# Hybrid decoder layer: where the transposes stand around the two output products of a token tile

## What is computed

```python
mix = merge_groups(h, om, att, g_m, g_a, w_out)      # rms_norm of both groups, then y @ w_out (1024 x 1024)
xp = layer_norm(DN_ALPHA * xp + mix, ln1_g, ln1_b)
...
logits = (xf @ w_router + b_router).astype(F32)      # 1024 x 32
top_v, top_i = lax.top_k(logits, TOP_K)
gates = jax.nn.softmax(top_v, axis=-1)
```

## Time and profile before

| | |
|---|---|
| time before, median of 3 runs | 1549.62 us (1548.44 to 1549.96) |
| the profiled execution, device time | 1550.05 us |
| its span, on which the trace's times stand | 1547.9 us |
| PE busy | 1383.3 us, 89% |
| DVE busy | 437.3 us, 28% |
| the loop over tiles 1 to 4 | 355.2 us to 434.9 us of the span |

### The profile page before, as it was taken

The page is one execution under the profiler, slowest core; times in us unless marked ns, Lnnn a source line. Parts: engine busy times, 40 slices in busy tenths (PEclk is TensorE's granted clock), DMA queues, the critical chain, the costliest instruction groups (busy, mean ns, idle before and its releaser), DMA issues.

```text
span 1547.9 us, 32726 instructions
## 1 busy us (share of the span) xinstructions
PE 1383.3 (89%) x12980; PEld 683.3 (44%) x12980; DVE 437.3 (28%) x1014; ACT 326.9 (21%) x758; POOL 311.8 (20%) x328
## 2 busy tenths in 40 slices
PE   7999899789879999988899999899998988999980
PEld 5778676574542433333334343233442333343330
DVE  2311534545564221221212212111321112211125
ACT  1102001361001322213222222221322212232120
POOL 5223200111231212111121112211112111122012
PEclk9999997669867999999999999999999999999996
DMA  9245000305046999999999999999999999999953
GB/s 303 61 89 122 21 35 23 97 25 211 28 151 237 398 409 402 410 413 410 411 402 405 412 409 410 404 408 408 402 412 405 409 408 405 405 401 408 417 205 115
DMA packets 100515, 460.85 MB, mean 298 GB/s; under 512 B 30482, under 2 KB 40862, under 8 KB 51200
## 3 DMA queue, kind: packets, MB, share of 16 engines
q1 hardware_dynamic: 81440, 426.48, 68.3%
q0 software_dynamic: 18336, 30.14, 7.8%
q10 hardware_dynamic: 592, 2.13, 0.4%
HBM read 442.21 MB, written 22.37 MB: 300 GB/s over the span
## 4 chain that ended last, share of the span: by engine, by line
PE 59%; DMA 20%; DVE 11%; SPq 5%; issue 3%; ACT 1%; POOL 0%; ACTq 0%; DVEq 0%; POOLq 0%
PE PS L1369 19%; DMA ring<-in_w_moe_dram 19%; PE PS L1391 14%; PE PS L1032 6%; PE PS L1044 6%; PE PS L1273 4%; SPq L489 3%; DVE mix L1927 2%; PE PS L1382 1%; PE PS L1351 1%; DVE qmT L1932 1%; DVE qmT L1934 1%; SPq L497 1%; PE PS L1361 1%; DVE qmT L1928 1%
## 5 line engine op out<-in xcount | busy, mean ns | idle before, releaser
L1369 PE MATMUL PS<-ring,mix 128*32 128x512 f32 x5376 | 605.1, 597 | 53.3 <-DMA ring<-in_w_moe_dram 42.4
L1369 PEld LDWEIGHTS PS<-ring,mix 128*32 128x32 f32 x5376 | 164.7, 110 | 453.3 <-issue 345.2
L769 POOL DMA_INDIRECT expert_rows<-mix,smalls x84 | 112.4, 1338 | 798.2 <-issue 511.4
L1927 DVE TENSOR_TENSOR mix<-PS,kn 128x512 f32<-128x512 f32 x84 | 58.1, 691 | 573.1 <-PE PS L1369 567.8
L960 ACT ACTIVATE mix<-PS,smalls 32x256 f32<-32x256 f32 x336 | 156.6, 466 | 179.5 <-PE PS L1391 176.4
L1391 PE MATMUL PS<-ring,mix 128*32 128x256 f32 x3328 | 187.0, 380 | 0.0
L1391 PEld LDWEIGHTS PS<-ring,mix 128*32 128x32 f32 x3328 | 104.7, 110 | 69.5 <-issue 0.5
L944 ACT COPY mix<-PS 128x512 f32<-128x512 f32 (+1 forms) x48 | 24.0, 535 | 466.0 <-PE PS L1361 466.0
L1032 PE MATMUL PS<-ring,xT 128*128 128x256 f32 (+1 forms) x400 | 97.7, 407 | 2.4 <-issue 2.2
L760 POOL DMA_INDIRECT mix<-x_rows,smalls x84 | 86.7, 1032 | 59.5 <-issue 52.9
L1044 PE MATMUL PS<-xT,ring 128*128 128x280 f32 x384 | 96.0, 413 | 0.0
(11 more groups left out here) (372 smaller groups left out, 1009.5 us busy)
## 6 DMA issues: line engine op xcount, KB each, us to landing
ring<-in_w_moe_dram SPq DMA_DIRECT2D x320, 1024.0 KB, 19.4
xT<-in_w_moe_dram SPq DMA_DIRECT2D x32, 1024.0 KB, 23.8
X<-in_w_moe_dram SPq DMA_DIRECT2D x32, 1024.0 KB, 27.2
ring<-in_w_in_dram SPq DMA_DIRECT2D x9, 1024.0 KB, 10.8
ring<-in_w_out_dram SPq DMA_DIRECT2D x4, 1024.0 KB, 4.8
X<-in_x_prompt_dram SPq DMA_DIRECT2D x4, 512.0 KB, 5.7
ring<-in_state_mlstm_C_dram POOLq DMA_DIRECT2D x1, 2048.0 KB, 16.3
ring<-in_w_in_dram SPq DMA_DIRECT2D x8, 256.0 KB
```

Of the source, the lines that this page charges most:

```text
L769: nc.gpsimd.indirect_dma_start(out=y_dram, out_offset=bass.IndirectOffsetOnAxis(ap=lists[a][0:32, g, 1:2].bitcast(U32), axis=0), in_=ysb[g ...
L1369: ins = mm(bank(BANK0[a] + g)[32 * t:32 * t + 32, :], xgT[XBUF[a][g]][:, P * (k % 2) + 32 * (k // 2):P * (k % 2) + 32 * (k // 2) + 32], sl ...
L1927: link(V.tensor_tensor(ht, bank(BANK0[a] + g), b1b, ALU.add))
```

## The change

Inside the loop, on PE, `turn_rows(i + 1)` moves from behind the second half product to between the two, and `turn_x1(i - 1)` moves from behind it to its middle, after four of its eight blocks. `logits(i - 1)` stays behind the second half. On DVE the two copies that answer to these, and with them `gates_by_expert`, are put in the same order: both copies stand ahead of the second half's residual. The two calls of `turned_x1` and `turn_x1` behind the loop stay. The count of instructions is the same; `project` takes the blocks to do as an argument and counts `op_mm` with the last of them.

```diff
-            def project(i, half):
+            def project(i, half, part=range(KT)):
...
                 else:
-                    for k in range(KT):
+                    for k in part:
                         ins = mm(bank(2 + 2 * (i % 2) + half), mixT[i % 2][:, k, :],
                                  rowpair((s0 + k // 2) % STREAM)[:, k % 2, 512 * half:512 * half + 512],
                                  start=(k == 0), stop=(k == KT - 1))
-                ins.then_inc(op_mm, 1)
+                if KT - 1 in part:
+                    ins.then_inc(op_mm, 1)
...
                 project(i, 0)
                 if i >= 2:
                     rank_tokens(i - 2)
-                project(i, 1)
                 if i < NT:
                     turn_rows(i + 1)
+                project(i, 1, range(KT // 2))
                 turn_x1(i - 1)
+                project(i, 1, range(KT // 2, KT))
                 logits(i - 1)
...
                 residual_half(i, 0)
                 if i >= 2:
                     give_places(i - 2)
+                if i < NT:
+                    turned_rows(i + 1)
+                turned_x1(i - 1)
+                if i >= 2:
                     gates_by_expert(i - 2)
                 residual_half(i, 1)
                 centre(i)
-                if i < NT:
-                    turned_rows(i + 1)
-                turned_x1(i - 1)
                 normalise(i)
                 choose(i - 1)
```

## The result

| | before | after |
|---|---|---|
| median | 1549.79 us (4 runs) | 1535.51 us (1533.29 to 1536.75, 4 runs) |
| ratio | | 0.9908, 95% interval 0.9891 to 0.9925 |
| profiled execution, device time | 1550.05 us | 1533.29 us |
| its span | 1547.9 us | 1531.1 us |

The gain of the medians is 14.3 us; 14.1 were forecast. One execution each of three kernels further down took far longer (2.1, 5.0 and 7.6 ms): the ratios leave it out, the medians printed there hold it and would be 0.3 to 1.4 us lower without it. The two profiled executions lie 16.8 us apart, so not all of their difference is the change. To see what is, I cut both traces at the same three events: the start of the first product of the loop, the end of the last one (read at the start of the next group on PE), and the start of the product with the second bias.

A forecast was written before the change was run, and what follows sets the result against it. The prediction took PE's 9.5 us of waits for DVE's copy of the turned X, and the clock lost with them, as the bound. Loop 13.17 - 0.30 breaks + 1.26 behind it = 14.1 us gained: median 1535.5, range 1533.3 to 1542.5.

The forecast's parts named there:

- The bound: PE before the logits: waits for DVE's copy of X; a full tile pays gap, half-clock logits and slow next product.
- Tile 1: First, small-logits turn of the loop on PE: loses only its gap, 1.89 us.
- Tile 2: Second turn of the loop on PE: 22.12 us becomes 17.51, 4.61 less.
- Tile 3: Third turn of the loop on PE: 23.60 us becomes 17.60, 6.00 less.
- Tile 4: Last turn of the loop on PE, to the end of its products: 15.80 us becomes 15.13, 0.67 less.
- Logits at full clock: A full tile's logits on PE without the gap: taken as 1.60 us, between bounds of 1.44 and 1.81.
- The allowance of 0.3 us for breaks: Four more breaks in the products on PE, each a fresh start of 0.05 to 0.1 us: 0.3 us lost.
- The waits in the middle: PE's transposes inside the second half product: wait 0 to 0.2 us in tile 4; rival of 1 us per tile, 1539.5, chance 0.05.
- Behind the last product: DVE's chain after the loop: copy of X leaves it, LayerNorm and router 1.26 us earlier, POOL's root stays hidden.
- The expert stage: After the router: everything later hangs on the last product and DVE's chain, so the shift counts in full.
- The fall of the clock: Rival on PE in tiles 2 and 3: broken-up products lose full clock, 6.9 us given back, 1542.4; chance 0.11, whole or part.
- The slower rival: PE stays at 0.50 through all products from the first break on: 45 us more, less the 14, 1580 us; chance 0.03.

## Why POOL's root took a microsecond longer

In before, and with only the rows moved, or only PE's order, a copy out of PSUM stood on DVE while POOL made the reciprocal root, and line 718 took 0.57 us in the full tiles. With only X moved it took 0.56, 0.56 and 0.57 us in the tiles whose copy of rows stands there, and 1.58 in the last, where there is none. In the change it is 1.56 to 1.58 in every full tile. The small tile, which never had a copy there, has 1.46 in both kernels. One more kernel keeps DVE still while POOL works.

```diff
                 link(V.tensor_scalar(nbias[0:r], bag[0:r, 0:1], -1.0, None, ALU.mult))
-                link(V.scalar_tensor_tensor(z, z, nbias[0:r], lng[0:r, :], ALU.add, ALU.mult))
                 dve.wait_ge(ln_pow, i + 1)
+                link(V.scalar_tensor_tensor(z, z, nbias[0:r], lng[0:r, :], ALU.add, ALU.mult))
```

> The change, but DVE waits for POOL's reciprocal root ahead of the first step of the LayerNorm instead of ahead of the second, so DVE touches no rows while POOL works. Theory (DVE's full-width step on SBUF slows POOL's line 718 from 0.57 us to 1.57, and so the copy from PSUM that used to stand there was a cover): line 718 takes 0.57 us in all four full tiles. DVE then waits about 0.9 us and does both steps of 1.28, 3.6 us from the statistics to x1_done where the change has 3.4, so the bias product starts 22.3 us after the last output product instead of 22.1. Rival (line 718 is slow for a reason of its own): 1.57 again, and 23.3 us.

Measured: 1533.62 us in one run. Line 718 takes 0.54 us for the small tile and 0.56 to 0.57 for the others, and the bias product starts 22.5 us after the last output product (417.69 to 440.17), where the change has 22.1. The rows of DVE in the last tile, then POOL's:

```profile
419.66 0.15 DVE L1770 TENSOR_SCALAR smalls<-smalls 128x1 f32<-128x1 f32 x1
420.67 1.33 DVE L1772 SCALAR_TENSOR_TENSOR X<-X,smalls,kmT 128x1024 f32<-128x1024 f32 x1 [0.86 <-POOL smalls L718]
```

```profile
419.99 0.57 POOL L718 TENSOR_TENSOR smalls<-smalls 128x1 f32<-128x1 f32 x1
```

The cause is shown: DVE's 1.28 us step that reads X and the LayerNorm's gain, both in SBUF, makes POOL's 0.57 us instruction wait one microsecond. The Trainium skill (SBUF — State Buffer, SBUF: two separate sides) says that a DVE instruction with two SBUF inputs and a GpSimd instruction that reads SBUF lock each other out for the length of the one that came first; the trace agrees: DVE's step starts first, at 419.50, POOL's at 419.64, and POOL's ends 0.43 us behind DVE's, after 1.57 us instead of 0.57. Waiting first avoids the lock but not the time: it costs 0.4 us more.

## Why the prediction was right, step by step

- **The bound.** The three prices of a full tile (gap, logits at half clock, slow start of the product) are all gone. Right, and shown by undoing the parts.
- **Tile 1.** 1.89 us forecast, 1.75 measured (17.91 before, 350.75 to 366.91 after).
- **Tile 2.** 17.51 us forecast, 17.60 measured (366.91 to 384.51).
- **Tile 3.** 17.60 forecast, 17.67 measured (384.51 to 402.18).
- **Tile 4.** 15.13 forecast, 15.17 measured (402.18 to 417.35).
- **Logits at full clock.** I took 1.60 from bounds of 1.44 and 1.81; they took 1.71 us. The upper bound halved the length of the row, 3.62; half of the time from its start to the next one's, 3.43 (391.83 to 395.26 in the earlier trace rows), is 1.71. The allowance of 0.3 us for breaks covered the difference: the loop came out at 66.60 where the forecast has 66.56. The single breaks were cheaper than the allowance: two half products and the transposes between them take 4.31 + 3.43 us (392.73 to 397.04 to 400.47), and 6.95 + 0.87 is 7.82, against 7.74 measured.
- **The waits in the middle.** The place that tile 4's transposes wait for was done at 412.86 and PE came to it at 413.01. The slack was 0.15 us, the forecast had a wait between 0 and 0.2. No wait shows in the trace. This is the step with the least room; in tiles 2 and 3 about 1.0 us is left. The copy of X was there 1.9 us before the logits (398.54 and 400.47 in tile 3) and not 1.2: it began 0.3 us into the last four blocks, not 0.9.
- **Behind the last product.** Here a step failed, though the forecast came out. The prediction read POOL's root as done 0.94 us behind the statistics "so it stays hidden". But 0.57 us was its time beside a copy out of PSUM, and the change takes just that copy away. The row of the small tile in the earlier trace rows already held the answer: there line 1771 waits 0.52 us for line 718, with no copy ahead. Mis-sized by 0.54 us: 0.73 gained instead of 1.26.
- **The expert stage.** Counted as shifting in full; it does, apart from the 1.2 us that its length grew by.
- **The rivals.** The fall of the clock did not come. Its cause was not excluded by the rows I gave, though: the logits three times over show that a busy PE can lose it. Its price was a little high: in before, the logits and the products behind them take 6.4 us more than at full clock, where I had 6.9. The waits in the middle came within 0.15 us. The slower rival did not occur either, but its row, the bias product at half clock, turned out to be worth 7.1 us in its stage, of which 4.9 reach the next.

That the medians differ by 14.3 us and the forecast by 14.1 is luck in the last microseconds. By the stretches of the two traces the change brings 13.6 us up to the bias product, 12.8 and 0.7, and loses 1.2 behind it. The medians add to that what chance gives: the runs of the change alone lie 3.5 us apart.

## What to carry to other kernels

Where two engines work through lists in order and one waits for the other's copy, move the producer's transposes into the middle of a long product and the copy ahead of the next thing that waits for that product; do both, since the first alone made this kernel about 10 us slower. Before you move an instruction away, look at what ran on other engines beside it: it may have been the cover of one of them. When a stretch is busy and still at half clock, look at the shape of its products before you look for idle time.

## What the runs showed of the hardware that I had not expected

- The granted clock fell from 1.00 to 0.50 3.9 and 3.3 us into 6.7 and 7.3 us of gapless logits (128 rows by 32 columns out), and from 1.00 to 0.50 inside a gapless product over 32 rows. It held at 1.00 over 3.5 us of float32 transposes between two half products, and over the 40 that open the kernel.
- The same product over 128 rows, 96 of them zeros in the gates, went from 0.50 to 1.00 within 3 us: 10.4 us for 20 instructions where 32 rows took 17.5.
- A gap of 2.21 us still lost the clock, as one of 2.60 did: 5.2 us above full clock for two tiles' logits and the products behind them, against 6.4.
- A DVE instruction with two inputs in SBUF held up a POOL instruction of 0.57 us by 1.0 us.
